# First attention: projection order of queries and gates swapped, and three of four sets of each turned by transfers and VectorE instead of TensorE

## The reference, cut to what matters

```python
h = rmsnorm(x, g_pre[i])
q, k, v, z = jnp.split(h @ w_in, [BRANCH, BRANCH + KV_A, BRANCH + 2 * KV_A], axis=-1)
scores = jnp.einsum('bnqhgd,bnkhd->bnhgqk', q, kb) * (HEAD_DIM ** -0.5)
scores = scores - slopes[:, :, None, None] * dist
p = jax.nn.softmax(jnp.concatenate([scores, sink_col], axis=-1), axis=-1)[..., :-1]
o = jnp.einsum('bnhgqk,bnkhd->bnqhgd', p, vb).reshape(B, S, BRANCH)
y = (o.astype(z.dtype) * jax.nn.silu(z)) @ w_out
x = x + rmsnorm(y, g_post[i])
```

## Time and profile before

| | |
|---|---|
| time, median of 3 runs | 1778.86 us (1778.46 to 1779.96) |
| profiled execution: its own time, its span | 1779.23 us, 1777.6 us |
| TensorE / VectorE / ScalarE / GpSimd busy | 99% / 71% / 50% / 10% |
| first attention, iterations 0 to 3 | 53.9 to about 279 us |
| one iteration of the loop | 56.2 us |

### The profile page before, as it was taken

How to read it: one execution, slowest core, us unless ns; L and a number is a source line. 1 busy time by engine, 2 the same in 40 slices (tenths; PEclk the granted TensorE clock), 3 DMA queues, 4 the chain that set the end, 5 groups by cost and what they waited for, 6 DMA issues and landing times.

```text
span 1777.6 us, 25074 instructions
## 1 busy us (share of the span) xinstructions
PE 1762.5 (99%) x8178; PEld 1447.4 (81%) x8178; DVE 1265.3 (71%) x1661; ACT 887.1 (50%) x1251; POOL 171.8 (10%) x313
## 2 busy tenths in 40 slices
PE   9999999999999999999999999999999999999998
PEld 7777778887888888888888888888888888888886
DVE  5677779777977877887778868777775655445445
ACT  6766674555444453544444545444444444444443
POOL 1011101010212312210000101000000000000000
PEclk9999999999999999999999999999999999999999
DMA  9778788555777879799998957999998766555554
GB/s 360 256 255 288 234 278 312 207 184 178 236 237 254 270 225 304 230 323 302 314 298 295 327 191 252 319 315 311 311 294 242 234 218 195 192 192 195 191 193 139
DMA packets 199662, 451.14 MB, mean 254 GB/s; under 512 B 19136, under 2 KB 30384, under 8 KB 199216
## 3 DMA queue, kind: packets, MB, share of 16 engines
q1 hardware_dynamic: 168080, 343.28, 59.3%
q0 software_dynamic: 31376, 107.04, 18.0%
q10 hardware_dynamic: 144, 0.03, 0.0%
HBM read 434.03 MB, written 12.06 MB: 251 GB/s over the span
## 4 chain that ended last, share of the span: by engine, by line
PE 90%; DVE 4%; DMA 3%; ACT 1%; issue 1%; SPq 0%; DVEq 0%; ACTq 0%
PE bank L1612 28%; PE bank L1614 28%; PE bank L1613 28%; DMA raw<-in_w_in_a 1%; DVE w_lo L1025 1%; DMA raw<-in_w_in 1%; DMA rope_ab<-rot 1%; PE bank L1782 1%; PE bank L1658 1%; DVE acc_a L1032 1%; PE bank L1765 1%; DVE rope_ab L1328 0%; PE bank L1871 0%; PE bank L1757 0%; PE bank L1877 0%
## 5 line engine op out<-in xcount | busy, mean ns | idle before, releaser
L1025 DVE TENSOR_TENSOR w_lo<-raw,w_hi 128x1024 fp32r<-128x1024 f32 x605 | 727.9, 1209 | 393.5 <-ACT w_hi L623 392.2
L623 ACT ACTIVATE w_hi<-raw 128x1024 fp32r<-128x1024 f32 x605 | 633.5, 1050 | 715.1 <-PE bank L1614 622.0
L1612 PE MATMUL bank<-w_hi,h_hi 128*128 128x512 f32 x2272 | 895.4, 394 | 3.4 <-DVE w_lo L1135 1.8
L1614 PE MATMUL bank<-w_hi,h_lo 128*128 128x512 f32 x2272 | 885.6, 390 | 0.0
L1613 PE MATMUL bank<-w_lo,h_hi 128*128 128x512 f32 x2272 | 885.0, 390 | 0.0
L1612 PEld LDWEIGHTS bank<-w_hi,h_hi 128*128 128x128 f32 x2272 | 426.7, 188 | 95.9 <-issue 7.0
L1614 PEld LDWEIGHTS bank<-w_hi,h_lo 128*128 128x128 f32 x2272 | 426.6, 188 | 90.1
L1613 PEld LDWEIGHTS bank<-w_lo,h_hi 128*128 128x128 f32 x2272 | 427.1, 188 | 85.4
L528 POOL DMA_DIRECT2D ada_raw<-in_w_ada x160 | 85.3, 533 | 794.6 <-DVE acc_a L1032 545.7
L1032 DVE SCALAR_TENSOR_TENSOR acc_a<-ada_raw,cond,acc_a 128x1024 f32<-128x1024 f32 x112 | 143.2, 1278 | 14.9 <-DMA ada_raw<-in_w_ada 14.9
L1032 DVE SCALAR_TENSOR_TENSOR acc_b<-ada_raw,cond,acc_b 128x1024 f32<-128x1024 f32 x48 | 64.3, 1339 | 1.4 <-DMA ada_raw<-in_w_ada 1.4
(11 more groups left out here) (211 smaller groups left out, 940.5 us busy)
## 6 DMA issues: line engine op xcount, KB each, us to landing
raw<-in_w_ff SPq DMA_DIRECT2D x256, 512.0 KB, 4.7
raw<-in_w_in SPq DMA_DIRECT2D x176, 512.0 KB, 4.6
ada_raw<-in_w_ada POOLq DMA_DIRECT2D x160, 512.0 KB, 5.6
raw<-in_w_in_a SPq DMA_DIRECT2D x69, 512.0 KB, 5.5
ada_more<-in_w_ada POOLq DMA_DIRECT2D x32, 512.0 KB, 6.1
raw<-in_w_out_a SPq DMA_DIRECT2D x32, 512.0 KB, 5.9
raw<-in_w_o SPq DMA_DIRECT2D x32, 512.0 KB, 4.9
raw<-in_w_moba SPq DMA_DIRECT2D x16, 512.0 KB, 4.8
```

The source lines that it names most:

```text
L623: act.activation(used(w_hi, turn, s), used(raw, turn, s), ACT.Copy).then_inc(hi_ready, 1)
L1025: dve.tensor_tensor(used(w_lo, turn, s), used(raw, turn, s), used(w_hi, turn, s).bitcast(F32), ALU.subtract).then_inc(lo_ready, 1)
L1612: pe.matmul(out_ap, hi, rhs_hi, start=start, stop=False)
L1614: return pe.matmul(out_ap, lo, rhs_hi, start=False, stop=stop)
```

## The change

Four things are changed together.

1. **Order of the projections.** Slots 0 to 7 of iterations 0 to 2 project the next queries (PAIR_B), slots 8 to 15 the gate of this group (PAIR_A). ScalarE empties the queries after slot 7 (`keep_queries`), the gate at the start of the next iteration (`z_sigmoid`), where VectorE finishes it (`gate_z` in slot 0, then `scale_z`).
2. **Turning without TensorE.** Queries of groups 1 to 3 and gates of groups 0 to 2 are written in a blocked order into `q1_tok`, moved in 16 transfers of 32 KB between blocks of 32 partitions into `post_gain` (12 from GpSimd's queue, 4 from SyncE's, each of these behind the load of a unit), and turned by VectorE in blocks of 32x32 (two instructions of 128x512). Queries are turned in slot 13, gates in slot 6 of the next iteration; there VectorE also multiplies them by the outputs. Queries 0 and the last gate stay on TensorE.
3. **Iteration 0 stands alone** on each engine; the loop has iterations 1 and 2. VectorE's added rows lie in slots 1 to 5, 7 to 12 and 14 of the loop and 2 to 5 of the last iteration.
4. In the last iteration ScalarE and VectorE split the gated outputs (`round_gated`, `low_h`) in slots 2 to 5, 7 and 8; the load of `post_gain` is issued later.

```diff
+        def move_qz(eng, done, j, i):
+            eng.dma_start(qz_back[j * QUAD:(j + 1) * QUAD, i * T * P:(i + 1) * T * P],
+                          quad_rows(q1_tok)[i * QUAD:(i + 1) * QUAD, j * T * P:(j + 1) * T * P]).then_inc(done, 16)
...
+            def last_of_gates(i, s):
+                if s == 1:
+                    gates_kept(sp, i)
+                if 1 <= s <= QUADS:
+                    move_qz(sp, qz_last, QUADS - 1, s - 1)
...
+                for s in range(UPT):
+                    col = i * CH + D + 2 * KV_COLS
+                    load(i * 2 + TURN_ZQ + 1, s, w_a[:, KG * s:KG * s + KG, col:col + CH])
+                    if i:
+                        last_of_gates(i - 1, s)
...
             def attn1_out(i, b):
                 act.wait_ge(o1_ready, i * 2 + b + 1)
+                if b == 0:
+                    act.wait_ge(og_ready, i * T + T)
...
+                if k == 0 and behind:
+                    act.wait_ge(o_gated, i * T)
                 if k < GROUP_A:
                     act.wait_ge(neg1_ready, i * GROUP_A + k + 1)
                     act.activation(s1[:, k % 2, 0:P], s1[:, k % 2, 0:P], ACT.Exp, bias=neg_cur[:, k, 0:1], scale=SCALE_A,
...
+            def attn1_turns(i, behind):
+                if behind:
+                    z_sigmoid(i - 1, i * 2 + TURN_ZQ - 1)
                 for s in range(UPT):
                     split(i * 2 + TURN_ZQ, s + AHEAD)
-                    attn1_slot(i, s, STEPS, SLOT_SUMS, SLOT_GATE)
+                    attn1_slot(i, s, STEPS, SLOT_SUMS, SLOT_GATE, behind)
+                keep_queries(i, behind)
...
+            def gate_moved(i):
+                moved(2 * i + 1)
+                for t in range(T):
+                    dve.transpose(z_t[:, :, t * P:(t + 1) * P], qz_returned[:, t]).then_inc(z_turned, 1)
+                dve.wait_ge(z_turned, i * T + T)
+                dve.wait_ge(o1_kept, i * 2 + 3)
+                dve.tensor_tensor(o_gated_t[:, bass.ds(i * 4, 4), :], z_t, o_t[:, :, :], ALU.mult).then_inc(og_ready, T)
...
+                if n == 0 and behind:
+                    gate_z(i - 1)
                 split(turn, n % UPT + AHEAD)
+                if n == 0 and behind:
+                    scale_z(i - 1)
+                if n == SLOT_Z and behind:
+                    gate_moved(i - 1)
...
+                if n == SLOT_Q and steps is STEPS:
+                    turn_queries(i)
```

More of the change, by code:

```diff
@@ L750, in keep_kv, with keep_queries @@
                     .then_inc(evicted[PAIR_A][t], 1)
+            def keep_queries(i, behind):
+                turn = i * 2 + TURN_ZQ
+                act.wait_ge(q1_t_ready, i * T + T)
+                if behind:
+                    act.wait_ge(z_turned, i * T)
+                for t in range(T):
+                    chunk_result(t, turn, turn)
+                    act.activation(q1_quad[:, t], in_quads(pair[PAIR_B][t][:, :]), ACT.Copy, scale=x_rstd[:, t:t + 1])\
+                        .then_inc(evicted[PAIR_B][t], 1)
             def keep_q1(turn):
@@ L791, in z_sigmoid, with attn1_slot @@
             def z_sigmoid(c, turn):
+                act.wait_ge(og_ready, c * T + T)
                 for t in range(T):
                     chunk_result(t, turn, turn)
-                    act.wait_ge(og_turned, c * T + t + 1)
-                    act.activation(z_silu[:, t, :], pair[PAIR_A][t][:, :], ACT.Sigmoid, scale=x_rstd[:, t:t + 1])\
-                        .then_inc(z_sig, 1)
-            def attn1_slot(i, n, steps, sums, gate):
+                    act.activation(z_silu[:, t, :], pair[PAIR_A][t][:, :], ACT.Sigmoid, scale=x_rstd[:, t:t + 1])                        .then_inc(z_sig, 1)
+            def attn1_slot(i, n, steps, sums, gate, behind):
                 if n == 0:
@@ L800, in attn1_slot @@
                 if n == 1:
-                    turn_q1(i)
+                    if not behind:
+                        keep_turned_q1()
+                    take_kv(i)
                 for k, at in enumerate(steps):
                     if at == n:
-                        attn1(i, k)
+                        attn1(i, k, behind)
                 if n == sums:
                     sink_share(i)
-                    z_sigmoid(i, i * 2 + TURN_ZQ)
+                    if steps is STEPS_LAST:
+                        z_sigmoid(i, TURN_Z_LAST)
                 if n == gate:
@@ L1795, in attn1_slot, with attn1_turns @@
                         attn1(i, k)
-                if n == turn:
+                if n == TURN_LAST and steps is STEPS_LAST:
                     turn_og(i)
-            pe.wait_ge(k1_ready, T)
-            with pe.Fori(0, CHUNKS - 1) as i:
-                for s in range(UPT):
-                    chunk_unit(i * 2 + TURN_ZQ, s, PAIR_A, i + 1)
-                    attn1_slot(i, s, STEPS, SLOT_TURN)
-                for s in range(UPT):
-                    chunk_unit(i * 2 + TURN_ZQ + 1, s, PAIR_B, i + 1)
-                    attn1_slot(i, UPT + s, STEPS, SLOT_TURN)
+            def attn1_turns(i, first):
+                for s in range(UPT):
+                    chunk_unit(i * 2 + TURN_ZQ, s, PAIR_B, i + 1)
+                    if s == 1 and first:
+                        turn_q1()
+                    attn1_slot(i, s, STEPS)
+                for s in range(UPT):
+                    chunk_unit(i * 2 + TURN_ZQ + 1, s, PAIR_A, i + 1)
+                    attn1_slot(i, UPT + s, STEPS)
+            pe.wait_ge(k1_ready, T)
+            attn1_turns(0, True)
+            with pe.Fori(1, CHUNKS - 1) as i:
+                attn1_turns(i, False)
             last = CHUNKS - 1
```

205 lines of the change are left out of this document (151 added, 54 removed).

## The result

| | before | after |
|---|---|---|
| time, median of 4 runs | 1778.99 us (1778.46 to 1779.96) | 1790.0 us (1789.01 to 1790.18) |
| ratio | | 1.0054, 95% interval 1.0042 to 1.0066 |
| span of the profiled execution | 1777.6 us | 1787.3 us |
| last matmul of TURN_Q to the transposes named below | 299.4 us | 309.1 us |
| from there to the end of the span | 1424.6 us | 1424.2 us |

What follows compares the result with a forecast made beforehand. TensorE, busy 99%, was taken as the bound: -5.3 + 0.75 + 1.65 + 2.55 + 3.2 = +2.85 us, forecasting 1781.7 us (+0.16%) against the median. The range ran from 1774.9 to 1785.5 us.

Steps and rivals of the forecast that it cites:

- What bounds the kernel: Whole kernel: a queue of matmuls on TensorE, busy 99%; only fewer TensorE instructions or new waits there move the time.
- A: TensorE's transposes: six sets of queries and gates removed at 0.88 us each, -5.3 us.
- B: Queries of groups 0 and 1 both fill PAIR_B; TensorE waits for ScalarE's copy of the first bank, +0.75 us.
- The landing time: SyncE's last transfer for slot 6: 5.1 us to landing, from the second attention, with 6.1 us kept as rival.
- C: Start of last iteration: two gates fill PAIR_A; TensorE waits for table load, sigmoid and VectorE's products, +1.65 us.
- D: First exponential of iterations 1, 2, 3: its table load starts only behind the mask, +0.85 us each, +2.55.
- weak premise: Table load ahead of the first exponential carries the wait for the mask; if it ran ahead, that cost is nothing.
- E: Gates turned on VectorE in slot 6 delay slot 9's turned probabilities: 0.9, 0.9, last iteration 1.35; 3.2 us.
- Rival 1: Slot 6's transfers are in time, the rest holds: sum -0.15, 1778.7 us; chance 0.15.
- Rival 3: Transfers in time and table loads ahead of their waits: sum -3.95, 1774.9 us, faster; chance 0.13.
- Rival 4: Last transfer in slot 6 lands late, at 6.1 us: sum +5.85, 1784.7 us, slower; chance 0.30.
- Rival 5: A drain of about 1380 ns behind each table load, by the skill's page: 1787.2 us; chance 0.02.

Runs made afterwards that it cites:

- run 1: Changed kernel with VectorE turning the queries in slot 15 instead of slot 13: 1783.8 us, ratio 1.0021.
- run 5: Changed kernel with SyncE's transfers issued two at a time behind two unit loads, the last two slots earlier: 1780.6 us, ratio 1.0007.
- run 4: Changed kernel with GpSimd's loads of the other product's rows in iterations 0 to 3 cut to 256 of 1024 columns: 1779.1 us, one execution.
- run 11: Changed kernel, last transfers two slots early, queries turned in slot 14, then 13, tables loaded ahead, their small buffers placed to move no other: 1776.7 us, ratio 0.9987.
- run 2: Changed kernel with sigmoid and exponential tables loaded ahead by small 128x1 activations: 1792.9 us, interval 1.0061 to 1.0087.
- run 6: Changed kernel with SyncE's last transfers two slots earlier and the queries turned in slot 15: 1779.8 us, ratio 0.9999.
- run 8: Changed kernel with each of a set's 16 transfers moving 4 KB instead of 32, plus a memset on GpSimd: 1783.6 us, one execution.
- run 7: Changed kernel with last transfers two slots earlier, queries turned in slot 15 and tables loaded ahead: 1780.8 us, interval 1.0002 to 1.0020.
- run 10: Kernel of run 5 with five 128x2 sigmoids between table load and sigmoid ahead of the last iteration, and an unused buffer: 1785.2 us.
- run 3: Changed kernel with queries turned in slot 15 and both tables loaded ahead: 1789.1 us, interval 1.0041 to 1.0066.
- run 12: Kernel before the change with an unused buffer of 8 bytes per partition added, nothing else: 1783.5 us, ratio 1.0026.

## Why the prediction was wrong, point by point

- **What bounds the kernel** and **A** were right. -5.2 for -5.3.
- **B** was right: 0.68 seen as the wait, 0.84 with the longer step.
- **"The turning of queries in slot 13 has three slots (over 8 us) before its scores" is the step that failed.** It asks when the result is wanted. It doesn't ask when the input lands, nor what is queued behind the turning on VectorE. I had done just that for slot 6 (issue at 133.85, landing 5.1 later, VectorE at 138.17) and not for slot 13. The last of SyncE's transfers was issued at 99.19 and landed some 9.8 us later, at 109.0, while VectorE was there at 104.87 (103.64 + 1.23). Runs 1 and 5 each show it: the turning two slots later gives 5.6 us of the stretch back, the transfers two slots earlier 8.0.
- **The landing time** was taken from another stage (5.1 and 6.1 us). For SyncE's it was 7.4 (median) in slots 8 to 12 and 6.2 in slots 2 to 6 of iteration 1, and the median hides what VectorE waits for: the last of the four took 9.8, 8.8 and 9.9 us in slots 8 to 12 of the three iterations. Run 4 shows that the bytes in flight are a large part of it (there it took 6.0, 4.6 and 4.6 us); the earlier trace rows couldn't tell that. In the Trainium skill, DMA: Bandwidth & Descriptors, section "Anatomy of one DMA — SWDGE (gpsimd) path" gives about 2.0 us and the bytes at 436 GB/s for GpSimd's path. Of all 96 transfers here the shortest, one of GpSimd's, took 1.7 us, the median was 4.7 and the longest, one of SyncE's, 9.9; no transfer of SyncE's took less than 3.4. So that price is met here only by the quickest of GpSimd's.
- **C** had the right chain with a wrong start: it let VectorE come to the gate's product at once. Two splits and a row stood in between, all late by the wait in slot 13. With the transfers in time (runs 4 and 5) the wait is 1.64, the 1.65 of the forecast. And the low clock behind it, 1.4 us, was in no case of mine.
- **D** had the right mechanism; each is 0.82 and 0.75 us where VectorE was in time, and 3.24 where it was late. That the load carried the wait was the "weak premise", and it held.
- **E** was right in iterations 1 and 2 within half a microsecond (1.38 and 1.39 for 0.9), with a wait of VectorE of 1.07 for the 0.8 forecast. In the last iteration, for which I had 1.35, nothing was lost: VectorE waited 0.13 us ahead of the turning there, and not at all in run 1, where that iteration starts 5 us earlier. SyncE's four transfers took 3.8 us (median) there. GpSimd loads 4 rows of the other product in it instead of 12; that this is the reason is only argued.
- **The rivals.** Rival 1 is run 4 (1779.1 for 1778.7), which is in part luck: it is a single execution, and its stretch is 0.9 us longer than before's where the rival's sum is -0.15. Rival 3, all in time and no table load, is run 11: 1776.7 for 1774.9. Of the 1.8 us between them 0.6 are what B, C and E cost more than in its sum (the steps of run 11 make -3.3, that sum -3.95), and 0.6 are before itself, at 1779.45 us beside run 11 in place of 1778.86; the rest I can't assign, and it is within the spread of the runs. Rival 4, transfers late in slot 6, pointed the right way, at the wrong slot. Rival 5, a drain behind each table load, can be left: the exponential at 124.57 begins 0.02 us behind the load's end.
- **A wait costs more than it lists.** 0.68 is 0.84, 0.15 is 0.21, 3.03 is 3.24 in the step between matmuls. Over the ten new waits in the stretch that is 1.4 us (13.4 for 12.0), which a sum of waits leaves out.

## What to carry to other kernels

A transfer between two pieces of work has two ends to check, not one: when its result is used, and whether it has landed when the engine that consumes it comes to it in program order, since everything queued behind stands too. Take the landing time from a stretch whose DMA engines are as full as the one in question, and the longest of the set and not its median, and put the consumer in the slot that the last transfer reaches, not two before and not later than needed. And when an experiment adds a buffer, lay it out where it moves no other, or the experiment measures the move.

## What the runs showed of the hardware that I had not expected

- **The clock of TensorE.** In the profiled executions it fell to its lower level for 3.4 us at the start of the last iteration, beginning between 0.5 us ahead of the end of the stand and 1.4 us behind it. The stands were of 4.38 us (after), 3.54 (run 2), 1.94 (run 1), 2.09 (run 6), 2.14 (run 8), 1.86 (run 7) and 1.95 us (run 10), and it stayed full behind those of 1.64 (runs 4 and 5). It also stayed full behind 3.03 us in slot 3 of iteration 1 (after) and behind 2.26 us at the start of the last iteration in run 3, where it had fallen earlier, behind a stand of 1.46 and one of 0.73 in slot 8. So the length of the one stand doesn't decide it alone; what else does is open. Each time costs 1.4 to 1.7 us on top of the stand. Nor does it fall in every execution of a kernel. No profiled execution with such a fall has a mean granted clock of 0.999, but nine of the eleven executions of run 6, six of the eleven of run 7, four of the twelve of run 1 and four of the eight of run 10 have. In run 7 those six took 1780.2 to 1780.8 us and the other five 1782.0 to 1786.1. So the profiled executions of runs 6, 7 and 10 show a fall that about half of the executions or more don't have.
- **Eight bytes.** The matmuls that read `o_hi` or `o_lo` took 395 to 396 ns in place of 389 when these lay 8 bytes further, and that stage took 2.6 us more; the kernel before was 4.1 us slower with them (run 12). The matmuls that read `h_hi` or `h_lo`, which lie ahead of the added buffer and didn't move, kept theirs (390 and 394 ns). In the Trainium skill, SBUF — State Buffer, section "Operand start alignment", a fp32 operand may start at any multiple of 4 bytes, and it says that this is about legality and not speed; here the speed did differ between two such starts.
